# Score products of two attentions: fp32 products against three fp32r products of split operands

## What is computed

```python
z      = einsum('bqhd,bshd->bhqs', q_sb, k_sb) * HEAD_DIM ** -0.5     # stick-breaking, 8 heads
logits = einsum('bqhd,bqkhd->bhqk', q_ds, k_sel) * HEAD_DIM ** -0.5   # indexed sparse, 8 heads
```

## Time and profile before

| | |
|---|---|
| time, median of 3 runs | 1436.6 us (1436.59 to 1437.49) |
| span of the profiled execution | 1435.6 us (no time of its own is listed for it beside the span) |
| PE busy | 1429.9 us (100%) |
| DVE busy | 1141.1 us (79%) |
| ACT busy | 843.4 us (59%) |
| POOL busy | 448.2 us (31%) |
| mean granted TensorE clock | 1.000 |
| DMA | 190 GB/s on average |

### The profile page before, as it was taken

One profiled execution on the slowest core, in us unless ns is written; L12 is line 12 of the kernel. 1 busy time (PEld: TensorE's weight loads), 2 busy tenths in 40 slices (PEclk: granted clock), 3 DMA queues, 4 the chain that ended last, 5 costly groups with the idle time before them and its releaser, 6 DMA issues.

```text
span 1435.6 us, 23655 instructions
## 1 busy us (share of the span) xinstructions
PE 1429.9 (100%) x7578; PEld 1226.4 (85%) x7578; DVE 1141.1 (79%) x1534; ACT 843.4 (59%) x1182; POOL 448.2 (31%) x495
## 2 busy tenths in 40 slices
PE   9999999999999999999999999999999999999999
PEld 8888888888888888888888888888888888888887
DVE  6778998886556556889967778778778778999998
ACT  6646667566767766666665455454554545465553
POOL 2310000423232213650015455655556555200000
PEclk9999999999999999999999999999999999999999
DMA  8665665665555555567666666666666665676664
GB/s 250 189 191 175 204 198 184 196 185 173 154 173 148 174 166 184 182 218 243 184 185 179 189 192 188 180 192 190 197 187 181 188 192 189 193 232 206 203 207 147
DMA packets 121064, 272.24 MB, mean 190 GB/s; under 512 B 10689, under 2 KB 10977, under 8 KB 121009
## 3 DMA queue, kind: packets, MB, share of 16 engines
q1 hardware_dynamic: 119936, 268.99, 61.2%
q0 software_dynamic: 896, 2.42, 0.6%
q10 hardware_dynamic: 176, 0.14, 0.0%
HBM read 269.42 MB, written 2.10 MB: 189 GB/s over the span
## 4 chain that ended last, share of the span: by engine, by line
PE 98%; DVE 1%; DMA 0%; issue 0%; ACT 0%; DVEq 0%; ACTq 0%
PE bank L2100 97%; PE bank L2154 1%; DVE lo L1223 0%; DMA y<-in_x 0%; PE bank L2369 0%; PE bank L2410 0%; DVE y L1770 0%; PE bank L2237 0%; PE bank L2173 0%; DVE msum L1242 0%; ACT hi L720 0%; DVE msum L1251 0%; DVE msum L1248 0%; PE bank L2215 0%; DVE y L1815 0%
## 5 line engine op out<-in xcount | busy, mean ns | idle before, releaser
L1106 DVE TENSOR_TENSOR lo<-raw,hi 128x1024 fp32r<-128x1024 f32 (+1 forms) x342 | 444.9, 1306 | 166.3 <-ACT hi L637 165.3
L637 ACT ACTIVATE hi<-raw 128x1024 fp32r<-128x1024 f32 (+1 forms) x342 | 359.6, 1054 | 270.8 <-PE bank L2100 262.9
L2100 PE MATMUL bank<-h2T,hi 128*128 128x512 f32 x1408 | 483.3, 394 | 0.0
L2100 PE MATMUL bank<-h2T,lo 128*128 128x256 f32 x1408 | 376.8, 278 | 0.0
L2100 PEld LDWEIGHTS bank<-h2T,hi 128*128 128x128 f32 x1408 | 257.9, 188 | 53.5
L2100 PE MATMUL bank<-hT,hi 128*128 128x512 f32 (+1 forms) x784 | 272.8, 395 | 0.0
L2100 PEld LDWEIGHTS bank<-h2T,lo 128*128 128x128 f32 x1408 | 264.5, 188 | 7.8
L2100 PE MATMUL bank<-hT,lo 128*128 128x256 f32 (+1 forms) x784 | 212.6, 281 | 0.0
L2064 POOL TENSOR_TENSOR u<-u,rms_row 128x256 f32<-128x256 f32 x88 | 120.7, 1372 | 184.9 <-DVE u L1622 165.9
L2100 PE MATMUL bank<-hi,ffT 128*128 128x512 f32 x576 | 177.4, 389 | 0.0
L2100 PEld LDWEIGHTS bank<-hT,hi 128*128 128x128 f32 (+1 forms) x784 | 143.9, 187 | 29.3
(11 more groups left out here) (301 smaller groups left out, 2031.7 us busy)
## 6 DMA issues: line engine op xcount, KB each, us to landing
raw<-in_w_up SPq DMA_DIRECT2D x176, 512.0 KB, 3.8
raw<-in_w_in SPq DMA_DIRECT2D x160, 512.0 KB, 3.6
raw<-in_w_down SPq DMA_DIRECT2D x88, 512.0 KB, 4.5
raw<-in_w_branch SPq DMA_DIRECT2D x32, 512.0 KB, 3.6
raw<-in_w_out SPq DMA_DIRECT2D x24, 512.0 KB, 4.8
raw4h<-in_w_in SPq DMA_DIRECT2D x8, 512.0 KB, 3.7
raw5h<-in_w_in SPq DMA_DIRECT2D x8, 512.0 KB, 4.0
y<-in_x SPq DMA_DIRECT2D x4, 512.0 KB, 6.5
```

What stands on the lines that cost most here:

```text
L637: act.activation(hi[s][:, 0:width], raw[s][:, 0:width], ACT.Copy)\
L1106: dve.tensor_tensor(lo[s][:, 0:width], raw[s][:, 0:width], hi[s][:, 0:width].bitcast(f32), ALU.subtract)\
L2100: return pe.matmul(o, l, r, start=start, stop=stop, skip_group_check=True)
```

## The change

The four staged tiles become one tile `qk_raw` of 4 times 256 columns (q and scaled k of the stick-breaking head, q and k of the sparse head). A new function of DVE, `qk_split(h)`, waits for the staging of head h, copies the whole tile to fp32r (`qk_hi`, 128x1024), waits for that copy, and subtracts (`qk_lo`, 128x1024). It runs once ahead of the loop for head 0 and then in the body of head h for head h + 1, behind the split of the last chunk (j = 7) and ahead of `column_sums`; the last head's body is taken out of the loop and has none. PE now waits for `qk_lo_done` instead of `staged_qk`, and each of the four score products becomes three fp32r products.

```diff
+            def qk_split(h):
+
+                dve.wait_ge(staged_qk, 3 * h + 3)
+                dve.tensor_copy(qk_hi[:, :, :], qk_raw[:, :, :]).then_inc(qk_hi_done, 1)
+                dve.wait_ge(qk_hi_done, h + 1)
+                dve.tensor_tensor(qk_lo[:, :, :], qk_raw[:, :, :], qk_hi[:, :, :].bitcast(f32),
+                                  ALU.subtract).then_inc(qk_lo_done, 1)
+
+            def gates_body(h, more):
                 for j in range(CPG):
                     split(C_GATES + AHEAD + j, h, CPG // SLOTS)
+                    if j == CPG - 1 and more:
+                        qk_split(h + 1)
...
-            with dve.Fori(0, NH) as h:
-                gates_body(h)
+            qk_split(0)
+            with dve.Fori(0, NH - 1) as h:
+                gates_body(h, True)
+            gates_body(NH - 1, False)
...
-                pool.tensor_copy(sb_q[:, :].unsqueeze(1), qkT[:, ds(h, 1), 0:S])\
+                pool.tensor_copy(qk_raw[:, 0:1, :], qkT[:, ds(h, 1), 0:S])\
                     .then_inc(staged_qk, 1)
...
-                        pe.wait_ge(staged_qk, 3 * h + 3)
+                        pe.wait_ge(qk_lo_done, h + 1)
 
                         pe.wait_ge(qkT_done, 8)
-                        mm(B[0][:, 0:S], sb_k[:, 0:P], sb_q[:, :], True, True)
-
-                        mm(B[0][:, S:KEYS], sb_k[:, P:S], sb_q[:, P:S], False, True)\
-                            .then_inc(z_full, 1)
-                        mm(B[1][:, 0:P], ds_qk[:, 0:P], ds_qk[:, S:S + P], True, True)
-                        mm(B[1][:, P:KEYS], ds_qk[:, P:S], ds_qk[:, S:2 * S], True, True)\
-                            .then_inc(logit_full, 1)
+                        for out_, left, right, first, full in (
+                                (B[0][:, 0:S], (1, 0, P), (0, 0, S), True, None),
+                                (B[0][:, S:KEYS], (1, P, S), (0, P, S), False, z_full),
+                                (B[1][:, 0:P], (2, 0, P), (3, 0, P), True, None),
+                                (B[1][:, P:KEYS], (2, P, S), (3, 0, S), True, logit_full)):
+                            (a, a0, a1), (b, b0, b1) = left, right
+                            mm(out_, qk_hi[:, a, a0:a1], qk_hi[:, b, b0:b1], first, False)
+                            mm(out_, qk_lo[:, a, a0:a1], qk_hi[:, b, b0:b1], False, False)
+                            i = mm(out_, qk_hi[:, a, a0:a1], qk_lo[:, b, b0:b1], False, True)
+                            if full is not None:
+                                i.then_inc(full, 1)
```

More of the change, by code:

```diff
@@ L247, in hybrid_layer @@
         part = [at(f"part{i}", [S], W0 + i * KB) for i in range(4)]
-        sb_q = at("sb_q", [S], W0 + 4 * KB)
-        sb_k = at("sb_k", [S], W0 + 5 * KB)
-        ds_qk = at("ds_qk", [2 * S], W0 + 6 * KB)
+        qk_raw = at("qk_raw", [4, S], W0 + 4 * KB)
+        qk_hi = at("qk_hi", [4, S], 44 * KB, f32r)
+        qk_lo = at("qk_lo", [4, S], 48 * KB, f32r)
         sb_v = at("sb_v", [TH, HD], W0 + 8 * KB)
@@ L443, in hybrid_layer @@
         staged_qk = sem("staged_qk")
+        qk_hi_done = sem("qk_hi_done")
+        qk_lo_done = sem("qk_lo_done")
         staged_v = sem("staged_v")
@@ L1481, in _ @@
                               ALU.is_gt, ALU.mult).then_inc(bias_raw, 1)
-            def gates_body(h):
+            def qk_split(h):
[5 more added lines that the diff above has]
+            def gates_body(h, more):
                 for j in range(CPG):
                     split(C_GATES + AHEAD + j, h, CPG // SLOTS)
+                    if j == CPG - 1 and more:
+                        qk_split(h + 1)
                     if j == 1:
@@ L1964, in stage_sb @@
             def stage_sb(h):
-                pool.tensor_tensor(sb_k[:, :].unsqueeze(1), qkT[:, ds(h, 1), S:2 * S],
+                pool.tensor_tensor(qk_raw[:, 1:2, :], qkT[:, ds(h, 1), S:2 * S],
                                    sb_scale[:, :].unsqueeze(1).to_broadcast([P, 1, S]),
                                    ALU.mult).then_inc(staged_qk, 1)
-                pool.tensor_copy(sb_q[:, :].unsqueeze(1), qkT[:, ds(h, 1), 0:S])\
+                pool.tensor_copy(qk_raw[:, 0:1, :], qkT[:, ds(h, 1), 0:S])\
                     .then_inc(staged_qk, 1)
             def stage_ds(h):
-                pool.tensor_copy(ds_qk[:, :].unsqueeze(1), qkT[:, ds(NH + h, 1), :])\
-                    .then_inc(staged_qk, 1)
+                pool.tensor_copy(qk_raw[:, 2:4, :].rearrange("p (n a) s -> p n (a s)", n=1),
+                                 qkT[:, ds(NH + h, 1), :]).then_inc(staged_qk, 1)
             with pool.Fori(0, 3) as i:
```

## The result

The kernel takes 1446.5 us (median of 5 runs, 1445.05 to 1446.88) against 1436.6 before (1436.59 to 1437.49): 1.0064 times as long, 95% interval 1.0054 to 1.0075. The forecast was 1443.9, with a range of 1440.5 to 1449.0. The direction and the place were as forecast; the loss is 9.9 us in the medians instead of 7.3.

The account below looks back on a forecast made before the run. PE, 98% of the chain, was taken to bound the kernel. Products +0.6, seven boundaries +5.7 and first head +1.0 made +7.3 us on 1436.6: 1443.9 us, range 1440.5 to 1449.0.

Parts of the forecast that it names:

- The stall at the boundaries: At seven boundaries between heads, PE waits 0.82 us each for column sums behind DVE's split: 5.7 us.
- The copy: DVE's copy of 1024 columns to fp32r in `qk_split`: taken as 0.70 us, 1.23 at the full price per column.
- the bias row: Profile row of DVE's one-operand bias, 384 columns in 0.352 us; basis for taking the copy at 0.70 us.
- Rival 1: DVE's copy runs at one element per cycle: +11.6 us in all, 1448.2 us; chance 0.17.
- The products: Twelve fp32r score products on PE take 1.38 us against 1.30 before: +0.6 us over 8 heads.
- The choice between 0.06 and 0.11 for a short product: Fp32r score products of 128 columns: 0.11 us taken, since a short product cannot cover the weight load that follows.
- rivals 3 and 4: Short fp32r products dearer than any row shows, 1448.7 us, chance 0.04; at 0.06 us with forecast stalls, 1441.4 us, chance 0.15.
- The first head: Ahead of the first score products PE waits for `qk_split(0)`: 1.0 us taken, 1.5 with the copy at full price.
- The sum: Adds products, seven boundaries and first head to +7.3 us, 1443.9 us; no later stage gives it back.

Follow-up runs that it names:

- the interleaved run: Against the change: split moved behind the column sums, each product of 128 columns behind one of 256; output not the layer's; 1439.7 us.
- run 26: Not a run label: <kept> says the kernel before, unchanged, was run 26 times in one set; 1436.3 to 1438.5 us.
- the block with fewer short products: Against the change: split moved behind the column sums, only 256-column products in fp32r, 128-column ones in fp32, second bank's outputs swapped; 1435.2 us.
- the run with the transpose: Against the change: split moved behind the column sums, one fp32 transpose of 128 columns added behind the twelve products; 1439.3 us.
- the half split with its fp32 products first: Against the change: only the stick-breaking pair split, in the same place; sparse attention's fp32 products first, six fp32r products last; 1439.8 us.
- the one with the short outputs last: Against the change: split moved behind the column sums, second bank's outputs swapped so products of 128 columns come last; 1440.1 us.

## Why the prediction was right, and where its size was off

**The stall at the boundaries**: right in cause, place and size. 0.80 us each against 0.82, seven of them, 5.6 us. Shown from both sides: half the work fits under the slack, a third instruction is paid in full, and behind the sums the same work costs no wait.

**The copy**: 0.686 us, against 0.70 from the bias row and 1.23 as the other end. Rival 1 is out. The copy of half the columns took 0.42 us, so 512 columns more cost 0.27 us, and 0.54 in the subtraction (0.69 and 1.23). The Trainium skill's rule (VectorE: DVE Perf Modes, What auto-detection actually checks), two elements a cycle for a single source with source and destination in SBUF, agrees with that: half the price per column, also for a copy to fp32r.

**The products**: 1.38 us as taken, +0.6 over the heads. The choice between 0.06 and 0.11 for a short product was right, and the interleaved run bears out its reason: rivals 3 and 4 are out. The Trainium skill's floor from weight loads (TensorE: Matmul & The Clock Gate, section LDWEIGHTS), some 107 ns for 128 columns, agrees: the loads start 0.11 to 0.12 us apart here. The Trainium skill's 81 ns for a stream of 128-column products (same page, Back-to-back issue gap) isn't reached.

**The first head**: 1.03 us against 1.0.

**What failed** is "The sum": it has no term for PE's other matmuls, and so lets them go on at their old pace. They don't: 31 pairs a head at 0.353 instead of 0.347 us, 0.19 us a head, 1.5 us in all. With it the stage should lose 5.6 + 0.6 + 1.0 + 1.5 = 8.7 us. The head shows it: 26.80 us against 26.6 forecast. So does the stage: from its first product to its last of 512 columns it takes 213.19 us (332.38 to 545.57) against 204.49 before (331.83 to 536.32), 8.7 more. That the time still lies inside the range owes something to luck: its upper part was held for rival 1, the dear copy, and no case had a term for the pace.

**The rest of the 9.9** is not the change's, as far as the runs show. The spans of the two profiled executions differ by 9.15 us: 8.7 in the stage, 0.55 ahead of it and -0.1 behind it. The heads stage already starts its last part 0.55 us later (the first transposes of `qn` at 262.33 against 261.77), where the two kernels do the same. That comes from the first 25 us, where the loads decide and did not fall alike: before, PE waits 0.39 us for `x`; after, it waits 0.79 us for the `lo` of a weight chunk, whose raw data ACT had waited 1.73 us for. Over all runs the first transposes of `qn` start between 260.7 and 262.7. The medians differ by 0.7 more. Five runs of the changed kernel lie in two groups, 1445.1 to 1445.3 and 1446.5 to 1446.9, and the median falls into the upper one; the kernel before, run 26 times in one set, goes from 1436.3 to 1438.5, with its median at the low end. The lower group is 8.4 to 8.7 us over before's median.

I also set the span of one execution against the median of others, as if 1.0 us lay between an execution's time and its span. In every execution with both on record 1.8 to 2.1 us do (1446.8 and 1444.8 for the profiled one of the change), so the profiled execution before, with its span of 1435.6, took about 1437.5 us by this estimate, 0.9 over the median.

## What to carry to other kernels

Work that is put on an engine with much idle time is free only where it stands ahead of nothing urgent: measure the slack of the next release behind it (1.22 us here), not the engine's busy share (79%), and move the work behind that release. Splitting an fp32 product into three fp32r ones saves time only where the product is wide: one of 256 columns goes from 0.43 to 0.35 us, one of 128 from 0.21 to 0.34, since each of the three brings its weight load. (These are estimates from 1.69 ns a column in fp32 and 0.12 and 0.11 us for an fp32r product; the block with fewer short products took the 1.16 us that they give within 0.02.)

## What was not expected of the hardware

A stream of fp32r matmuls of 512 and 256 columns in turn has two steady paces, 0.347 and 0.353 us a pair, with the same instructions, a granted clock of 1.00 and no wait. At the faster pace the starts repeat every pair (0.230 and 0.117 us); at the other they repeat every third pair (0.241, 0.120, 0.235, 0.114, 0.232, 0.118). Behind the score products the pace of the first pairs lasts for all 31, up to the next other instructions on PE. In this stretch it was always 0.347 where the block ends with fp32 products (before, and three variants), and 0.353 in nearly every head where it ends with fp32r ones, in whatever order these stand; the exceptions are the first head of the interleaved run and the second of the run with the transpose, at 0.347 behind the same instructions as in the other heads.

Elsewhere the kind of the product ahead does not settle it. The branch stage stands behind fp32 value products in all kernels and has the longer time in three. In two of these, the half split with its fp32 products first and the one with the short outputs last, the chunks behind the fp32 transposes of the first head go at 0.353 too, and at 0.347 in all later heads. All kernels, the one before too, fall into the slower pace once in the feed-forward stage, for some 20 us. Why is open. The exact moment at which the stream begins is a rival left standing: no run was made to vary that alone.
